# A fused conv / gated-linear-attention decoder block: the second block's norm is staged early, and its projections go between the first block's stages

## The reference

```
u = rms_norm(h, norm_mix_g) @ w_in                # 1024 -> 2576
c_val, c_gate, q, k, v, g, gate_lr = split(u)
y_conv = silu(layer_norm(causal_depthwise_conv31(c_val * sigmoid(c_gate)) + conv_b))
log_a  = log_sigmoid(gate_lr @ w_gate2 + gate_b) / 16
o      = gated_linear_attention(q, k, v, decay = exp(cumsum(log_a)))   # chunked, 4 heads
y_gla  = rms_norm_per_head(o) * silu(g)
h = h + concat(y_conv, y_gla) @ w_out
h = h + (silu(rms_norm(h) @ w_gate) * (rms_norm(h) @ w_up)) @ w_down   # width 2816
out = rms_norm(h, norm_final_g)                                        # meta rows dropped
```

## Time and profile before

| | |
|---|---|
| median of 3 runs | 1608.6 us (1606.13 to 1612.18) |
| the profiled execution's own time | 1602.56 us |
| span of its slowest core (core 3) | 1601.0 us (all cores 1589.0 to 1601.0) |
| PE busy | 1493.6 us, 93% of the span, 8450 matmuls and transposes |
| DVE, ACT, POOL busy | 801.0, 560.6, 223.1 us |
| granted TensorE clock, mean | 0.979 on core 3 |
| chain that ended last | PE 80%, DMA 9%, issue 3%, SP's queue 3%, DVE 3%, ACT 2% |
| DMA | 279.42 MB, mean 175 GB/s |

### The profile page before, as it was taken

One profiled execution on the slowest core, in us unless ns is written; L12 is line 12 of the kernel. 1 busy time (PEld: TensorE's weight loads), 2 busy tenths in 40 slices (PEclk: granted clock), 3 DMA queues, 4 the chain that ended last, 5 costly groups with the idle time before them and its releaser, 6 DMA issues.

```text
span 1601.0 us, 26625 instructions; the slowest of 8 cores (1589.0 to 1601.0 us)
## 1 busy us (share of the span) xinstructions
PE 1493.6 (93%) x8450; PEld 697.8 (44%) x8450; DVE 801.0 (50%) x1775; ACT 560.6 (35%) x863; POOL 223.1 (14%) x323
## 2 busy tenths in 40 slices
PE   5838999979999999999899999999999999999997
PEld 2423444434445344444444443444434444444443
DVE  5545356444365544656336562555526554365533
ACT  4354442223432345232442334423344234423211
POOL 3220142110140103101030000300003010210000
PEclk9968999999999999999999999999999999999999
DMA  9964689888867854447634576336653475544542
GB/s 191 246 232 107 148 176 190 185 234 240 203 151 215 240 159 140 152 147 236 165 128 119 178 231 163 130 119 225 196 155 127 148 256 158 139 145 153 199 161 93
DMA packets 79799, 279.42 MB, mean 175 GB/s; under 512 B 10784, under 2 KB 11168, under 8 KB 79664
## 3 DMA queue, kind: packets, MB, share of 16 engines
q1 hardware_dynamic: 55584, 192.13, 39.5%
q0 software_dynamic: 23472, 85.01, 21.9%
q10 hardware_dynamic: 608, 0.60, 0.1%
HBM read 250.49 MB, written 41.94 MB: 183 GB/s over the span
## 4 chain that ended last, share of the span: by engine, by line
PE 80%; DMA 9%; issue 3%; SPq 3%; DVE 3%; ACT 2%; DVEq 0%; POOL 0%; ACTq 0%; POOLq 0%
PE ps L629 53%; PE ps L1231 17%; PE ps L836 4%; DMA wring<-wsc 3%; SPq L757 3%; DMA rep<-vT 3%; PE ps L620 2%; DMA h<-xin 1%; DMA wring<-wpack 1%; ACT xn_tm L605 0%; DMA out<-h 0%; PE ps L859 0%; PE ps L1134 0%; PE ps L862 0%; PE ps L1098 0%
## 5 line engine op out<-in xcount | busy, mean ns | idle before, releaser
L629 PE MATMUL ps<-x2T,wring 128*128 128x512 bf16 x2752 | 618.1, 381 | 21.5 <-DMA wring<-wsc 11.1
L629 PEld LDWEIGHTS ps<-x2T,wring 128*128 128x128 bf16 x2752 | 264.1, 98 | 350.8 <-issue 48.0
L1231 PE MATMUL ps<-wring,actT 128*128 128x512 bf16 x1320 | 297.0, 379 | 1.3 <-DMA wring<-wpack 1.3
L1210 DVE SCALAR_TENSOR_TENSOR ftmp<-ftmp,ps 128x512 f32<-128x512 f32 x176 | 120.2, 686 | 252.4 <-ACT ftmp L1209 251.5
L1209 ACT ACTIVATE ftmp<-ps 128x512 f32<-128x512 f32 x176 | 104.8, 595 | 296.8 <-PE ps L629 266.1
L1231 PEld LDWEIGHTS ps<-wring,actT 128*128 128x128 bf16 x1320 | 126.9, 98 | 147.1 <-issue 1.8
L629 PE MATMUL ps<-xT,wring 128*128 128x512 bf16 x736 | 163.8, 379 | 2.3 <-ACT xT L623 2.3
L1212 DVE SCALAR_TENSOR_TENSOR actT<-ftmp,ps 128x512 bf16<-128x512 f32 x176 | 120.3, 687 | 64.2 <-PE ps L629 60.4
L629 PE MATMUL ps<-wring,yT 128*128 128x512 bf16 x512 | 117.4, 384 | 0.1
L629 PEld LDWEIGHTS ps<-xT,wring 128*128 128x128 bf16 x736 | 71.5, 98 | 88.5 <-issue 4.2
L629 PE MATMUL ps<-wring,xT 128*128 128x512 bf16 x448 | 101.8, 379 | 0.0
(11 more groups left out here) (192 smaller groups left out, 1353.6 us busy)
## 6 DMA issues: line engine op xcount, KB each, us to landing
wring<-wsc SPq DMA_DIRECT2D x318, 512.0 KB, 4.4
wring<-wpack POOLq DMA_DIRECT2D x52, 512.0 KB, 8.4
wsc<-wring POOLq DMA_DIRECT2D x38, 512.0 KB, 8.3
rep<-vT SPq DMA_DIRECT2D x112, 136.1 KB, 6.4
out<-h POOLq DMA_DIRECT2D x28, 512.0 KB, 7.3
h<-xin POOLq DMA_DIRECT2D x24, 512.0 KB, 10.8
h<-xin SPq DMA_DIRECT2D x8, 512.0 KB, 9.9
rep<-vT SPq DMA_DIRECT2D x32, 67.9 KB, 13.4
```

The source lines that it names most:

```text
L629: ins = e.matmul(pt_ap, lhsT=lhs(kc), rhs=rhs(kc), start=(kc == 0), stop=(kc == KC - 1))
L1210: P.add("dve", lambda e: e.scalar_tensor_tensor(out=th[:], in0=th[:], scalar=1.0, in1=pg[:], op0=ALU.add, op1=ALU.mult), R=[Bpg, Bth], W=[ ...
L1231: ins = e.matmul(ps[t][:], lhsT=actT[:, j, t * 128:(t + 1) * 128], rhs=wd3[:, j - 4 * s_, :], start=(j == 0), stop=(j == NJ - 1))
```

## The change

Six edits go together.

1. Where the second block's input goes early. The norm of the second block writes its four normalised tiles into the memory of `x2T` (`stage`, which is free until the first feed-forward part) instead of two rotating tiles. All four norms are one unit. The input tiles `h1_2` and `h1_3` are loaded when the first conv gate matmul has been done; before, all four waited for the K projection.
2. The homes move, since `x2T` and two of the `h1` tiles are no longer free: W_V lies in `h1_0`, `h1_1`, W_K in the second half of `yT`, W_Q and W_G in `actT`. Three of the four feed-forward tiles that were loaded at the start now come later, into the `actT` homes when W_Q and W_G have been used and stored.
3. `plan` is new: the first norm unit of the second block after Q; then keys, scores, state, the output gate G, the conv; then the second block's transposes and three of its conv gates ahead of the attention output, the statistics and the layer norm; the rest as before. The merge of the first feed-forward part with the second mixer begins at once (0.0 for 0.15).
4. In the first block's second norm the 1/sqrt is Ln and Exp on ACT (`table`).
5. The Newton chains are one DVE instruction shorter (`rsq_col` 6 for 7, `rsq_row` 8 for 9), everywhere.
6. Small moves in the first block: `k_tm` is evacuated by ACT, the attention's squares go into `csb`; and `schedule` keeps a DMA time for each issuing engine instead of one for all.

```diff
-        dma_free = 0.0
+        dma_free = {e: 0.0 for e in self.ENGS}
...
-        whome += [x2T[:, 4 * i:4 * i + 4, :].rearrange("p a n -> p (a n)") for i in range(2)]
-        whome += [h[1][t][:].bitcast(BF16) for t in range(NT)]
+        whome += [yT[:, 4:8, :].rearrange("p a n -> p (a n)")]
+        whome += [h[1][t][:].bitcast(BF16) for t in range(2)]
...
+            x2f = x2T[:].rearrange("p k n -> p (k n)")
+            stage = [(x2f[:, t * D:(t + 1) * D], Buf(f"stage{t}")) for t in range(NT)]
...
-            FIRST = (10, 11, 4, 5, 6, 7, 12, 13, 8, 9, 0, 1, 2, 3)
-            EXTRA = (14, 15, 16, 17)
+            FIRST = (9, 10, 4, 5, 6, 7, 8, 11, 12, 13, 0, 1, 2, 3)
+            EXTRA = (14, 11, 12, 13)
...
-                for i, sl in enumerate(FIRST + EXTRA):
+                for i, sl in enumerate(FIRST + EXTRA[:1]):
...
+            def rsq_col(stt, Bst_, scale, eps):
+                a, y, t_ = stt[:, 1:2], stt[:, 2:3], stt[:, 3:4]
...
+                for k in (3.0, 12.0):
+                    P.add("dve", lambda e: e.scalar_tensor_tensor(out=t_, in0=y, scalar=a, in1=y, op0=ALU.mult,
                                                                   op1=ALU.mult), R=[Bst_], W=[Bst_])
+                    P.add("dve", lambda e, k=k: e.scalar_tensor_tensor(out=y, in0=t_, scalar=k, in1=y, op0=ALU.subtract,
+                                                                       op1=ALU.mult), R=[Bst_], W=[Bst_])
...
+            def norm(ht, Bht, gt, slot, dst=None, table=False):
+                if dst is None:
+                    i = nxt("xn", 2)
+                    dst = (xn_tm[i][:], Bxn[i])
+                xn, Bx = dst
...
+                if table:
+                    y = stt[:, 1:2]
+                    P.add("act", lambda e: e.activation(out=y, in_=stt[:, 0:1], func=AF.Ln, scale=1.0 / D, bias=RMS_EPS),
+                          R=[Bs_], W=[Bs_])
+                    P.add("act", lambda e: e.activation(out=y, in_=y, func=AF.Exp, scale=-0.5), R=[Bs_], W=[Bs_])
+                else:
+                    y = rsq_col(stt, Bs_, 1.0 / D, RMS_EPS)
...
-                                W=[Bh[hs][t]], dkey=f"x1_{t}" if front else f"h{hs}_{t}", after=pace if front else ())
+                                W=[Bh[hs][t]], dkey=f"x1_{t}" if front else f"h{hs}_{t}", after=[P.all[pace[0]]] if front else ())
...
-                    xni[0] = norm(h[hs][0], Bh[hs][0], gmix, 0)
+                    for t in range(NT if front else 1):
+                        xni[t] = norm(h[hs][t], Bh[hs][t], gmix, t, stage[t] if front else None)
...
-                    sq, Bsq = mtm()
+                    if meta and t == 0:
+                        Bcs2.rd += Bcs.rd + [Bcs.lw]
+                    sq, Bsq = (csb[:, tt, :], (Bcs, Bcs2)[tt]) if meta else mtm()
...
-                        xni2[t] = norm(h[hs][t], Bh[hs][t], gffn, t)
+                        xni2[t] = norm(h[hs][t], Bh[hs][t], gffn, t, table=meta)
...
-            plan = [("all", 0, fn) for fn in m0["a"] + m0["o"] + m0["conv"]]
-            plan += [("two", 1e3, fn) for fn in f1[:8]]
-            plan += [("six", 0, fn) for fn in m0["stat"] + m0["ln"]]
+            plan = []
+            for k in ("a", "dec", "mk", "k", "q"):
+                plan += [("all", 0, fn) for fn in m0[k]]
+            plan += [("two", 1e3, fn) for fn in f1[0:1]]
+            for k in ("kt", "s0", "kv", "s1", "g", "conv"):
+                plan += [("all", 0, fn) for fn in m0[k]]
+            plan += [("two", 1e3, fn) for fn in f1[1:8]]
+            for k in ("o", "stat", "ln"):
+                plan += [("six", 0, fn) for fn in m0[k]]
             plan += [("two", 1e3, fn) for fn in f1[8:14]]
             plan += [("six", 0, fn) for fn in m0["late"]]
...
-                steps = merge(f, m, 0.15, 0.93) if m else [fn for _, fn in f]
+                steps = merge(f, m, 0.15 if b else 0.0, 0.93) if m else [fn for _, fn in f]
```

More of the change, by code:

```diff
@@ L174, in schedule @@
             if o.dma:
-                dma_free = max(dma_free, free[e]) + o.nbytes / DMA_RATE
-                end = dma_free + (5.0 if e == "pool" else 3.0)
+                dma_free[e] = max(dma_free[e], free[e]) + o.nbytes / DMA_RATE
+                end = dma_free[e] + (5.0 if e == "pool" else 3.0)
             else:
@@ L600, in newton_row @@
-                return y
-            def norm(ht, Bht, gt, slot):
-                i = nxt("xn", 2)
-                stt, Bs_ = stn[:, slot, :], Bst[slot]
[L605 to L608, removed]
+                    P.add("dve", lambda e: e.tensor_tensor(out=t_, in0=t_, in1=a, op=ALU.mult), R=[B_], W=[B_])
@@ L671, in _ @@
                         transp(xni[t], xT[:, :, t * 128:(t + 1) * 128], BxT[t])
+                        if front:
+                            for B_ in Bx2T:
+                                B_.rd.append(P.all[-2])
                     if meta:
@@ L838, in mmconv @@
                             return ins
-                        P.add("pe", mmconv, R=Brep[c] + [Bwcv], W=[Bpcv], after=[stt["g"]] if meta else ())
+                        P.add("pe", mmconv, R=Brep[c] + [Bwcv], W=[Bpcv])
                         P.add("act", lambda e: e.activation(out=ycv[c], in_=v2(pcv[:]), func=AF.Identity, bias=cvec[:, 0, c:c + 1]),
@@ L997, in _ @@
                     P.add("pe", ktr, R=Bk + [Bident], W=[Bpt])
-                    P.add("dve", lambda e: e.tensor_copy(out=k_tm[:], in_=ptb), R=[Bpt], W=[Bktm])
+                    if meta:
+                        P.add("act", lambda e: e.activation(out=k_tm[:], in_=ptb, func=AF.Copy), R=[Bpt], W=[Bktm])
+                    else:
+                        P.add("dve", lambda e: e.tensor_copy(out=k_tm[:], in_=ptb), R=[Bpt], W=[Bktm])
                     if not meta:
@@ L1116, in o_tile @@
                         return
[L1117 removed]
+                    if meta:
+                        Bcs.rd += [Bcs2.lw] + Bcs2.rd
+                    y = rsq_row(v, Bsto[pr], 1.0 / 128, RMS_EPS)
                     for i in range(2):
@@ L1188, in mixer @@
                 if meta:
-                    return {k: [fn for (_, fn), k_ in zip(units, keys) if k_ == k] for k in ("a", "o", "conv", "stat", "ln", "late")}
+                    return {k: [fn for (_, fn), k_ in zip(units, keys) if k_ == k]
+                            for k in ("a", "dec", "mk", "k", "q", "g", "kt", "s0", "kv", "s1", "o", "conv", "stat", "ln", "late")}
                 return units
@@ L1292, in final @@
                               R=[Bh[hs][t]], W=[Bxn[i], Bstf])
-                    y = newton_row([stf[:, k, :] for k in range(6)], Bstf, 1.0 / D, RMS_EPS)
+                    y = rsq_row([stf[:, k, :] for k in range(6)], Bstf, 1.0 / D, RMS_EPS)
                     for t in range(NT):
```

78 lines of the change are left out of this document (36 added, 42 removed).

## The result

The changed kernel took 1593.3 us (median of 4 runs), the kernel before 1607.4 beside it; the ratio is 0.989, 95% interval 0.985 to 0.993. On another chip the ratio was 0.986 (0.985 to 0.988). 1597 was predicted, so the time was right; the place was not. (Ratios leave out executions in which one die ran at a lower clock.)

The account below looks back on a forecast made before the run. TensorE was taken as busy nearly throughout, except around 60 to 165 us, where the change must earn its time. 18.5 - 4.1 - 3 + 0.3 = 11.7 us off 1602.6 gives 1590.9; with the median 6.0 higher, 1597 (1584 to 1615).

Parts of the forecast that it names:

- The shorter chains ... elsewhere they are off the path: One DVE instruction less per rsqrt chain: 0.3 us gained at the span's end, nothing elsewhere.
- Gain of 18.5 us: Second block's 64 gate and value matmuls (14.0 us), a transpose, z and a wait leave the stretch behind the output projection.
- (a): First block's decay factor of the keys, on ACT behind input tiles 2 and 3: 58.3 us instead of 48.91.
- (b): First copies into `rep` start at 53.7 us, not 47.0; input tile 0 lands at 76, scores come at 80.5.
- (c): Second 16 copies land at 91 us, not 83; state and conv quarters follow, conv ends near 102, not 100.45.
- (d): Attention output behind the conv delays the statistics: nothing to 16 us, 5 taken; output projection starts at 131.5, not 125.11.
- Given back, 3 us: First feed-forward part must have its weights, refilled from the output projection's end: between nothing and 10 us, 3 taken.
- A: Rival: input tiles late, each 11.5 us after the other, tile 3 at 71; gain gone, about 1608 us; chance 0.20.
- B: Rival: input tiles 2 and 3 land early, at 48; conv ends 4 to 5 us earlier, 1592 us; chance 0.15.
- C: Rival: first feed-forward part ends no earlier than its weight transfers, 10 us lost for 3, 1604 us; chance 0.10.
- D: Rival: SP held at input tile 0 by W_V's store; if until 90 us, 1619 us or so; chance 0.12.
- the likeliest case: The forecast itself: 1597 us, own range 1588 to 1605 from the attention output's place and the weights; chance 0.43.

Follow-up runs that it names:

- b_chains: The kernel before with only the shorter rsqrt chains put in; ratio 0.986 (0.983 to 0.989) to the kernel before.
- a_tiles_later: The changed kernel with the planner's landing time of the second block's four input tiles 5 us longer; ratio 0.981 (0.978 to 0.983) to the kernel before.
- before_again: The kernel before, unchanged, run again on another chip for a trace beside the changed kernel; ratio 1 by definition.

## Why the prediction was right in time and wrong in place

- **"The change has to earn its time between about 60 and 165 us"**: this step failed. At the second mark, 3.1 us (5.2 on the other chip) were won; five blocks then won 10.3 (17.1: 955.0 down to 937.9). The page of before has 18.0 us of waits for `rep` in the conv's row, and the order of one steady block would have shown 66 become 90; I went by the busy slices.
- **"The shorter chains ... elsewhere they are off the path", 0.3 us**: the term that was missed. `b_chains`, which has them alone, is 1.4% faster (0.986). It changes DVE's work and the planner's costs at once, so what each gave is not separated; that the waits for `rep` halved says that the place of the conv is the larger part. I did not price `dma_free` at all, and it gave 0.8% (0.992).
- **Gain of 18.5 us**: right in kind. 64 gate matmuls stand ahead and none behind; TensorE's idle time from 60 to 165 us fell from 35.5 to 22.2 us on core 3, 13.3 for "some 15".
- **(a), (b)**: right. Tiles 2 and 3 at 52.6 and 56.6 (52.5, 57), the key factor at 57.6 (58.3), copies from 54.3 (53.7), tile 0 issued at 65.5 (64.5) and there at 77.1 (76), last query at 79.3 (80), scores at 80.1 (80.5).
- **(c)**: the path was right, copies, then state products, then three quarters of the conv; mis-sized by 3 us. The conv ended at 105.1, not 102. The second copies took SP 19.45 us, not 10.7, and the last landed near 92.5 (91); from there to the second quarter 4.9 us passed (4), and the three quarters took 7.6 (7).
- **(d)**: mis-sized by 5 us. From the conv to the end of the last layer-norm product 32.4 us passed, not 29.5, and z with its wait held the output projection for 2.2 more. So the loss was 12.5 us for 4.1. Why the layer norm took longer was not tested.
- **Given back, 3 us**: 18.5 - 12.5 = 6.0, and 5.4 were left at the first mark, so 0.6. In the next part core 3 waits 5.6 us at once for a weight tile, as it did before (5.4).
- **Table loads**: one more than before, not two (39.75, 41.66 and 43.39 us; before 39.58 and 43.03), and hidden; ACT waits 7.1 us for tile 2 behind them.
- **Rivals**: A and B fall by the tiles' times (neither 59.5 and 71 nor both at 48), C by the marks of a_tiles_later, D because SP issued tile 0 without standing at it. What happened was none of them: a first block between the likeliest case and A, by another mechanism, and a steady state that was not on the list.

Two errors of opposite sign, 8.4 us too hopeful in the first block and 10 to 17 us blind in the rest, gave a time 4 us from the one measured. That is luck; the sum did not hold what made the gain.

## What to carry to other kernels

A change of a planner's costs is a change of every block: compare the order of one steady block before and after, and multiply what moved there by the number of blocks, before pricing the prologue. A wait of 3 us does not show in a busy share of 93%; the list of waits has it, with its count. Add up all waits, before and after: here 13.4 us of waits for copies went, and 9.8 us of waits for the next thing in line came. Where a planner takes a transfer for early, its consumer stands at the head of an in-order engine; planning four tiles 5 us later was worth 0.6% here (0.986 to 0.981).

## What the runs showed of the hardware

A long wait is often paid twice. Windows of the kernel before (before_again, core 3) around the wait of 5.53 us; the last three columns are the granted clock, DMA share and GB/s:

```profile
798.50:804.00 5.50, 0.02 (x1) 0.00 (x0) 1.62 (x4) 1.21 (x2) 0.07 (x1) 0.75 1.02 260
804.00:810.00 6.00, 5.95 (x66) 2.55 (x67) 0.00 (x0) 1.36 (x3) 1.44 (x3) 0.66 0.16 64
810.00:830.00 20.00, 20.00 (x138) 8.70 (x137) 6.88 (x10) 9.01 (x14) 5.89 (x6) 1.00 0.34 107
```

The granted clock was down (0.66, so in part at the lower of its two levels, 1.2 GHz) in the 6 us behind it, and the conv's first 64 matmuls took 5.62 us; behind a wait of 2.53 us one block earlier they took 3.65. So removing this wait was worth 7.5 us, not 5.5. It is not so behind every wait: of 42 such waits of over 1 us on the eight cores of that run (from the first mark on), 28 were followed by 64 matmuls that took 4.9 to 6.5 us and 14 by ones that took 3.65; the first kind lasted 2.2 to 5.6 us, the second 1.2 to 3.0. The Trainium skill (TensorE: Matmul & The Clock Gate, "HAM oscillation — how this bites in real kernels") says that waits for transfers can drop TensorE to its lower clock; the row agrees. And SP spent 19.45 us on issuing 16 copies that took 10.97 in the first half, without a wait of its own in the trace; in a_tiles_later the second half took 13.21. What holds the issues up, the runs do not tell.
